# Ten of eleven FFN slabs by the seven-product scheme, with DRAM sums and four steps at other places

## The reference

```python
def reference(x, ...):
    x = first_block(x, p, norm_w, w_in, ...)
    return second_block(x, p_2, attn_norm_g_2, w_in_2, ...)

def first_block(...):                 # D_MODEL 2048, SEQ 256
    u = rmsnorm(h, norm_w[l])
    proj = jnp.einsum('bsd,dc->bsc', u, w_in[l])
    h_a = mlstm_chunkwise(q_a, k_a, v_a, i_pre, f_pre)
    y_a = jax.nn.sigmoid(ml_o) * h_a * jax.nn.silu(ml_z)
    h_b = hgrn2_chunkwise(q_b, k_b, logf_b, i_b)
    y_b = h_b * jax.nn.silu(hg_g)
    h = h + jnp.einsum('bsc,cd->bsd', y, w_out[l])
    gate = jax.nn.sigmoid(jnp.einsum('bsd,de->bse', rmsnorm(h, pe_norm_w[l]), w_pg[l]))
    h = h + gate * e
    ...
def second_block(...):                # FFN_HIDDEN 5632
    proj = h @ w_in[i]
    y_a = chunked_spatial_gating(u, v_sgu, w_s[i], b_s[i])
    y_b = stick_breaking_attention(q, k, v_att)
    merged = jax.nn.sigmoid(g_a) * (y_a @ w_up_a[i]) + jax.nn.sigmoid(g_b) * (y_b @ w_up_b[i])
    x = x + merged @ w_o[i]
    hid = rmsnorm_2(x, ffn_norm_g[i]) @ w_ffn_in[i]
    gate, up = hid[..., :FFN_HIDDEN], hid[..., FFN_HIDDEN:]
    x = x + (jax.nn.silu(gate) * up) @ w_ffn_out[i]
    ple = p[i] @ w_ple[i]
    x = x + jax.nn.sigmoid(rmsnorm_2(x, ple_norm_g[i]) @ w_ple_gate[i]) * ple
```

## Time and profile before

| what | value |
|---|---|
| median of three runs (lowest, highest) | 1894.37 us (1893.72, 1894.42) |
| the profiled execution | 1893.05 us |
| its span, first to last instruction | 1891.3 us |
| mean granted clock | 0.999 |
| busy: PE, DVE, ACT, POOL | 1877.2, 1471.8, 1140.8, 130.4 us |
| DMA, mean | 283 GB/s moved |

### The profile page before, as it was taken

How to read it: one execution, slowest core, us unless ns; L and a number is a source line. 1 busy time by engine, 2 the same in 40 slices (tenths; PEclk the granted TensorE clock), 3 DMA queues, 4 the chain that set the end, 5 groups by cost and what they waited for, 6 DMA issues and landing times.

```text
span 1891.3 us, 23371 instructions
## 1 busy us (share of the span) xinstructions
PE 1877.2 (99%) x9018; PEld 1641.9 (87%) x9018; DVE 1471.8 (78%) x1591; ACT 1140.8 (60%) x1417; POOL 130.4 (7%) x156
## 2 busy tenths in 40 slices
PE   9999999999999999999999999999999999999998
PEld 8888888888888888888888888888888888888887
DVE  6889776655666677778888657988998999898865
ACT  7556445555566556566766455666766676666553
POOL 4000011000001100000000000000000000000000
PEclk9999999999999999999999999999999999999999
DMA  9799898999989879998797886788878887987653
GB/s 392 267 284 310 274 309 272 330 347 327 309 290 312 271 269 299 321 315 278 295 313 247 330 256 239 254 311 284 276 254 320 280 271 257 327 260 249 219 188 130
DMA packets 86815, 535.95 MB, mean 283 GB/s; under 512 B 10416, under 2 KB 11184, under 8 KB 40752
## 3 DMA queue, kind: packets, MB, share of 16 engines
q1 hardware_dynamic: 72736, 458.69, 63.3%
q0 software_dynamic: 13824, 75.50, 20.6%
q10 hardware_dynamic: 144, 0.26, 0.0%
HBM read 529.69 MB, written 105.38 MB: 336 GB/s over the span
## 4 chain that ended last, share of the span: by engine, by line
PE 90%; DVE 5%; DMA 3%; issue 1%; ACT 1%; POOL 0%; SPq 0%; ACTq 0%; DVEq 0%; POOLq 0%
PE acc L1359 44%; PE acc L1364 22%; PE aux L1724 12%; PE aux L1728 6%; DVE wlo L2556 2%; PE aux L1338 2%; DMA ple<-in_w_ffn_in 1%; DVE wlo L1876 1%; PE aux L1431 1%; DVE ple L2551 1%; DMA ple<-in_w_in 1%; DMA raw<-summed 1%; PE aux L1805 0%; ACT whi L928 0%; ACT whi L1177 0%
## 5 line engine op out<-in xcount | busy, mean ns | idle before, releaser
L1876 DVE TENSOR_TENSOR wlo<-raw,whi 128x1024 fp32r<-128x1024 f32 x512 | 623.8, 1226 | 296.4 <-ACT whi L928 288.4
L928 ACT ACTIVATE whi<-raw 128x1024 fp32r<-128x1024 f32 x511 | 534.0, 1054 | 449.8 <-PE acc L1364 414.1
L1359 PE MATMUL acc<-whi,actA_hi 128*128 128x512 f32 x892 | 344.0, 386 | 0.7 <-ACT whi L928 0.7
L1359 PE MATMUL acc<-whi,actA_lo 128*128 128x512 f32 x892 | 339.1, 380 | 0.0
L1359 PE MATMUL acc<-whi,actB_hi 128*128 128x512 f32 x796 | 304.5, 383 | 0.2 <-DVE actB_lo L2673 0.2
L1359 PE MATMUL acc<-whi,actB_lo 128*128 128x512 f32 x796 | 301.7, 379 | 0.0
L1177 ACT ACTIVATE whi<-ple 128x1024 fp32r<-128x1024 f32 x192 | 201.0, 1055 | 139.4 <-PE acc L1364 55.6
L2556 DVE TENSOR_TENSOR wlo<-ple,whi 128x1024 fp32r<-128x1024 f32 x192 | 230.2, 1220 | 31.3 <-ACT whi L1177 28.5
L1364 PE MATMUL acc<-wlo,actA_hi 128*128 128x512 f32 x892 | 229.1, 379 | 0.0
L1364 PE MATMUL acc<-wlo,actB_hi 128*128 128x512 f32 x796 | 204.4, 379 | 0.0
L2556 DVE TENSOR_TENSOR wlo<-raw,whi 128x1024 fp32r<-128x1024 f32 x144 | 174.2, 1220 | 30.6 <-ACT whi L1177 28.9
(11 more groups left out here) (366 smaller groups left out, 2377.0 us busy)
## 6 DMA issues: line engine op xcount, KB each, us to landing
raw<-in_w_in SPq DMA_DIRECT2D x108, 1024.0 KB, 7.3
raw<-in_w_ffn_out SPq DMA_DIRECT2D x44, 1024.0 KB, 6.9
summed<-in_w_ffn_in POOLq DMA_DIRECT2D x36, 1024.0 KB, 11.6
raw<-in_w_ffn_in SPq DMA_DIRECT2D x72, 512.0 KB, 7.9
ple<-summed SPq DMA_DIRECT2D x24, 1024.0 KB, 4.9
raw<-summed SPq DMA_DIRECT2D x48, 512.0 KB, 5.4
ple<-in_w_ffn_in SPq DMA_DIRECT2D x18, 1024.0 KB, 6.9
ple<-in_w_ffn_in POOLq DMA_DIRECT2D x36, 512.0 KB, 9.9
```

Of the source, the lines that this page charges most:

```text
L928: act.activation(whi[:, g % RING], raw_piece(g), ACT.Copy).then_inc(hi_ready, 1)
L1359: pe.matmul(acc2(n)[:, t, :], act[x][:, k + c, t * P:(t + 1) * P], woven(whi, g, c), start=(p == 0 and c == 0 and x == 0), stop=False)
L1876: dve.tensor_tensor(wlo[:, g % RING], raw_piece(g), whi[:, g % RING].bitcast(F32), ALU.subtract)\
```

## The change

- **FFN.** Ten slabs (1 to 10) go by the seven-product scheme, slab 0 alone is standard. There are 13 seven-product slabs for 12 and 860 pieces for 848: 364 short ones (336) and 496 standard (512). F0 has 12 standard pieces (gate 0 and half of up 0), b3 8, b4 4, b5 to b11 8 each, and the last, b12, 12. b3 begins at g 452, b4 at 488, b5 at 520. Out pieces come as slab 0 alone ("out1"), pairs (1, 2) to (7, 8), slab 9 alone and 10 alone in the tail. `S_UPTO` sets by hand how many short pieces have been done by each standard piece in the first two blocks. Fills may stand behind a short piece.
- **DRAM sums.** 52 for 48. The four entries at g 277 to 289 are gone; those at every sixth piece from g 419 are twelve, to g 485, for four. POOL issues those from 443 on behind the power of the FFN's norm, in F0 and b3.
- **mLSTM rows.** Two of the four matmuls with `sel` come one piece later.
- **hB** is multiplied one piece later, **u_product** of uB 2 at five pieces after its slab for three.

```diff
@@ -91,24 +91,30 @@
     (1, [("gB", 0), ("uB", 0, 0, 0, 2)]),
     (2, [("uB", 0, 0, 2, 4), ("uA", 1), ("uB", 1)]),
     (3, [("uA", 2), ("uB", 2)]),
-    (1, [("gate", 3), ("up", 3, 0, 0, 2)]),
-    (2, [("up", 3, 0, 2, 8), ("out", (0, 1), 0, 0, 4)]),
-    (4, [("out", (0, 1), 0, 4, 8), ("out", (0, 1), 2, 0, 6)]),
-    (5, [("out", (0, 1), 2, 6, 8), ("out", (3, 2), 0)]),
-    (6, [("out", (3, 2), 2), ("out", (4, 5), 0, 0, 2)]),
-    (7, [("out", (4, 5), 0, 2, 8), ("out", (4, 5), 2, 0, 4)]),
-    (8, [("out", (4, 5), 2, 4, 8), ("out", (6, 7), 0, 0, 6)]),
-    (9, [("out", (6, 7), 0, 6, 8), ("out", (6, 7), 2)]),
-    (10, [("out", (8, 9), 0), ("out", (8, 9), 2)]),
+    (1, [("up", 0, 0, 4, 8), ("out1", 0, 0), ("out1", 0, 1)]),
+    (2, [("out1", 0, 2), ("out1", 0, 3)]),
+    (3, [("out", (1, 2), 0)]),
+    (4, [("out", (1, 2), 2)]),
+    (5, [("out", (3, 4), 0)]),
+    (6, [("out", (3, 4), 2)]),
+    (7, [("out", (5, 6), 0)]),
+    (8, [("out", (5, 6), 2)]),
+    (9, [("out", (7, 8), 0)]),
+    (10, [("out", (7, 8), 2), ("out1", 9, 0), ("out1", 9, 1)]),
 ]
-FILLS = [(0, 1, 0, 0, "d"), (0, 2, 0, 1, "d"), (1, 1, 1, 0, "d"), (1, 2, 1, 1, "d"), (2, 7, 3, 0, "e"), (2, 9, 3, 1, "e"),
...
+S_UPTO = {M_GROUPS: (0, 4, 8, 18, 21, 24, 28, 28), M_GROUPS + 1: (3, 10, 18, 28)}
+FILLS = [(0, ("s", 12), 0, 0, "e"), (0, ("s", 16), 0, 1, "e"), (1, 3, 1, 0, "e"), (1, ("s", 22), 1, 1, "e"),
...
-HID_T = {0: 0, 1: 1, 2: 1, 3: 0, 4: 0, 5: 1, 6: 0, 7: 1, 8: 0, 9: 1, 10: 2}
-HID_S = [0, 1, 0, 2, 1, 0, 2, 1, 0]
+HID_T = {j: j % 2 for j in range(10)}
+HID_T[10] = 2
+HID_S = [0, 1] * 5
 OUT_LAST = 10
+LAST_OUT = [(9, 2), (9, 3)] + [(OUT_LAST, q) for q in range(4)]
 S_GROUPS = len(BLOCKS)
 S_ORDER = [(m, q) for m in ("M1", "M2", "M7", "M5") for q in range(4)] \
     + [("M6", 0), ("M6", 1), ("M3", 0), ("M6", 2), ("M3", 1), ("M6", 3), ("M3", 2), ("M3", 3)] + [("M4", q) for q in range(4)]
@@ -188,7 +196,7 @@
         self.g_ffn = self.g
         self.first["F0"] = len(self.slabs)
         self.pair = self.g // 2
-        for x in self.unit("gate", 0) + self.unit("up", 0):
+        for x in self.unit("gate", 0) + self.unit("up", 0, 0, 0, 4):
             self.add_std(x, 4)
         self.g_block = self.g_ffn + 10
         self.pair = 0
@@ -197,7 +205,7 @@
         self.plan_s_loads(range(M_GROUPS, S_GROUPS))
         self.g_tail = self.g
         self.pair = 0
-        tail = [("ple", 0, q, 0) for q in range(4)] + [("out1", OUT_LAST, q, p) for q in range(4) for p in range(2)]
+        tail = [("ple", 0, q, 0) for q in range(4)] + [x for j, q in LAST_OUT for x in self.unit("out1", j, q)]
         for x in tail:
             self.add_std(x, 4)
         self.after.update({(S_GROUPS, t): self.g_tail + t for t in range(len(tail))})
@@ -215,7 +223,7 @@
         for t, x in enumerate(std):
             self.after[c, t] = self.g
             self.add_std(x, 2)
-            upto = max(0, min(28, t * 28 // (len(std) - (1 if c == M_GROUPS - 1 else 3))))
+            upto = S_UPTO[c][t] if c in S_UPTO else min(28, t * 28 // (len(std) - (1 if c == M_GROUPS - 1 else 3)))
             while done < upto:
                 self.add_s(c, done)
                 done += 1
@@ -464,7 +472,6 @@
         summed = nc.dram_tensor("summed", (4 * S_GROUPS, P, 4 * COLS), F32, kind="Internal").ap()
         SUM_AT = [int(24 + SUM_STEP * i) for i in range(int(116 // SUM_STEP) + 1)] + [144 + 8 * i for i in range(7)]
         SUM_AT += [199 + int(5.4 * i) for i in (0, 1, 2, 3, 8, 9, 10, 11, 12, 13)]
-        SUM_AT += [PLAN.g_plan + 1 + 4 * i for i in range(4)]
         SUM_AT += [PLAN.g_out + 11 + 6 * i for i in range(4 * S_GROUPS - len(SUM_AT))]
 
         acc = ctx.enter_context(nc.psum_tensor("acc", [P, 4, COLS], F32))
@@ -897,7 +904,7 @@
                                 pool.wait_ge(lo_ready, S_AT[c, before, q] + 1)
                                 pool.dma_start(r1[:, q], s_weights(c, what, q), accum_op=ALU.add).then_inc(sem(f"r1_added{q}"), 16)
                 if name == "ffn":
-                    add_in_dram(len(SUM_AT))
+                    add_in_dram(len([g for g in SUM_AT if g < PLAN.g_ffn]))
                 pool.wait_ge(pow_in, i + 1)
                 pool.tensor_tensor(rstd[:, i, 0:n], var[:, i, 0:n], minus_half[:, 0:n], ALU.pow).then_inc(pow_out, 1)
@@ -1490,12 +1497,13 @@
                         ins = pe.transpose(bank(u)[:, x * 8 + t * 4:x * 8 + t * 4 + 4], hrow[:, row, t * P:(t + 1) * P],
                                            ident[0:4, 0:4])
                 ins.then_inc(aux_full, 1)
-                for i in range(2):
-                    u = AUX[("bc", i)]
-                    free(u)
-                    for h in range(2):
-                        ins = pe.matmul(bank(u)[:, h * S:(h + 1) * S], sel[:, 2 * i + h, :], hrow[:, 3, :], start=True, stop=True)
-                    ins.then_inc(aux_full, 1)
+
+            def ml_rows_spread(i):
+                u = AUX[("bc", i)]
+                free(u)
+                for h in range(2):
+                    ins = pe.matmul(bank(u)[:, h * S:(h + 1) * S], sel[:, 2 * i + h, :], hrow[:, 3, :], start=True, stop=True)
+                ins.then_inc(aux_full, 1)
 
             def ml_scores():
                 pe.wait_ge(sem("ml_qk"), 2)
@@ -1550,6 +1558,9 @@
                         ml_gates_tr()
                     if (s, p) == (10, 7):
                         ml_cols()
+                        ml_rows_spread(0)
+                    if (s, p) == (11, 0):
+                        ml_rows_spread(1)
                     if (s, p) == (11, 4):
                         ml_scores()
                     for h in range(4):
@@ -2245,7 +2256,7 @@
                         if w == L0 + 27:
                             dve.wait_ge(sem("ss_hB"), half + 1)
                             variance(f"hB{half}", HG_E)
-                        if w == L0 + 30:
+                        if w == L0 + 31:
                             powered(dve, f"hB{half}")
                             x = ob[:, :, half * 512:(half + 1) * 512].rearrange("p t (h c) -> p t h c", h=4)
                             link(dve.tensor_tensor(x, x, per_head(f"hB{half}").unsqueeze(3).to_broadcast([P, T, 4, P]), ALU.mult))
@@ -2628,7 +2639,8 @@
                         gate_taken(PLAN.ffn_slab[role, j, 0])
                 for j in range(4):
                     for role in ("uA", "uB"):
-                        if g == slab_end(role, j) + (2 if slab_end(role, j) in PLAN.block_end else 3):
+                        last = slab_end(role, j)
+                        if g == last + (2 if last in PLAN.block_end else 5 if (role, j) == ("uB", 2) else 3):
                             u_product(role, j)
                 for c in range(M_GROUPS):
                     if g == S_AT[c, "M2", 3] + 3:
```

10 lines of the change are left out of this document (6 added, 4 removed), and 8 rows, old and new, of the table FILLS.

## The result

The changed kernel takes 1963.83 us (median of five, 1956.09 to 1970.65) for 1893.72 us, a ratio of 1.0372 (95% interval 1.0352 to 1.0391). It is 70 us slower; the forecast was 27 us slower, and the range ended at 1950. The profiled execution is the fastest of the five: 1956.09 us with a span of 1954.2, 62.9 more than before.

What follows compares the result with a forecast made beforehand. PE was taken as the bound (1877.2 of 1891.3 us busy), DMA close by. 1893.05 - 9.8 (small gains) + 28 (late sums) + 8.4 (M4 additions) = 1919.7, plus 1.3 for the median: 1921 us; range 1902 to 1950.

Steps and rivals of the forecast that it cites:

- the two mechanisms: DMA work of the late sums holding up F0 to b4, and M4 additions landing late in b5 to b11.
- the small terms: Five gains: fewer matmuls 5.2, clock 1.8, hB 0.9, u_product 0.9, early sums 1.0; together -9.8 us.
- the M4 additions: b5 to b11: 1.3 us less cover for the last addition, about 1.2 us new stall a block, +8.4 us (2 to 14).
- Fewer matmuls: Whole kernel: 8136 matmuls for 8160, 24 x 0.216 us less on PE, -5.2 us in full.
- Clock, hB, u_product: Half clock at 276.4 to 279.8 us gone, -1.8; PE waits near 161 and 1028 us gone, -0.9 each.
- Early sums gone: First merge block: 32.6 us of DMA work leaves, the 0.66 us stall and half the other waits go, -1.0 us.
- The late sums: F0 to b4's end: eight sums make DMA's work 164.8 us against PE's 136.6, +28 us (20 to 38).
- DVE's form_lo against M1 in b3: Short pieces M1 meet form_lo at b3's beginning: up to 2.9 us, counted as zero because DMA holds it up there anyway.
- The rivals: Queues not full, 1895 us (0.07); neither term holds, 1887 (0.10); queues block each other, 1946 (0.09); clock still falls, +1.8.
- (3): SP stands at copies waiting for sums, loads behind them blocked, DMA share 0.92: +53 for +28, 1946 us, chance 0.09.
- the forecast of +16: F0 to b4 at the skill's 358 GB/s: 54.5 MB take 152 us, late sums' term +16, time 1909 us.

Runs made afterwards that it cites:

- three_orders: The kernel before with only the spread mLSTM rows, hB one piece later and u_product of uB 2 two pieces later: 1892.04 us, ratio 0.9987.
- before_late: The kernel before with only the sums moved: the four at g 277 to 289 gone, eight at 419 to 461; 1898.71 us, ratio 1.0027.
- no_add: The changed kernel without its last eight DRAM sums and without the M4 additions in the FFN blocks: 1900.11 us, ratio 1.0035.
- after_m4: The changed kernel, all sums in place, with b5 to b11's standard pieces moved, two between the last M4 addition's issue and use: 1935.42 us, ratio 1.0210.

## Why the prediction was right or wrong

**Slower, and where:** right. b3 to b4 and the seven blocks behind are the places that it named, and it named the two mechanisms. It was wrong in size, 27 us for 70. By the profiled executions 36.3 us are missing: b5 to b11 lost 27.2 more than before where the forecast had 8.4, b3 and b4 43.2 where it had 28, and the small terms came to 2.3 less than their 9.8. The other 6.4 us are the median, which stands 7.7 above this execution and not 1.3. So two terms were too small, the M4 additions by most.

**Fewer matmuls, -5.2:** right; the stages without stalls (b12, J) are at their matmuls' time.

**Clock, hB, u_product, -3.6:** the stalls and the half clock are gone, but the whole was -2.0 (three_orders). **Early sums gone, -1.0:** too small; the first merge block won 2.4 us in the changed kernel and 2.7 in before_late. Of the smaller stalls behind the one shown, which the term took at half, one of 0.2 us is left.

**The late sums, +28:** right in size: 25.8 us by profiles, 31.3 by medians, of which the copies alone are 0.6. That the size came out is in part luck. I set the work against PE's time up to b4's end. In fact DMA is full (1.01) through F0, b3 and the first stall of b4, and then partly idle, so that b4 has a share of 0.83 as a whole: what waits are b4's first loads, not its last, and what DMA has free behind them gives nothing back. A sum to b3's end, with 130.8 us of DMA work (20 MiB of loads, four additions, eight sums) to 89 of PE, would have shown the wait where it came, though at 42 us it is too large for it: 19.5 us were lost to b3's end. The clock's falls, 1.9 us in b3 and 3.1 in b4, weren't in the sum. The share of 0.80 that it gives for b3 before is that of 1163 to 1240 us, a quarter of it F0; b3 itself was at 0.85.

**The M4 additions, +8.4:** the term that failed. b5 to b11 lose 27.7 us, for 0.5 before. Without the late sums they lose 32.6, of which 25.1 go with the additions (no_add), and b4, which I had left out, has 7.2. The last addition of b7 in the timeline of the changed kernel, POOL, PE, ACT and PE:

```profile
1487.43 0.86 POOL L905 DMA_DIRECT2D ple<-in_w_ffn_in  x1 [2.62 <-DVE wlo L2567]
...
1496.44 0.59 PE L1739 MATMUL aux<-wlo,actA_hi 128*128 128x512 f32 x2
...
1498.94 1.06 ACT L1184 ACTIVATE whi<-ple 128x1024 fp32r<-128x1024 f32 x1 [3.98 <-DMA ple<-in_w_ffn_in]
...
1500.05 0.48 PE L1735 MATMUL aux<-whi,actA_hi 128*128 128x512 f32 x1 [3.02 <-ACT whi L1184]
```

The last two matmuls ahead, 0.216 us each, end at 1496.87, which is 9.4 us behind the issue. In the earlier trace rows (it is the last of b3's four additions that they show, not the first, as their heading says) the same distance was 11.75 us, since PE's last two matmuls ahead were these, ending at 1237.72, and M4's first came at 1237.87:

```profile
1237.29 0.59 PE L1728 MATMUL aux<-wlo,actA_hi 128*128 128x512 f32 x2
```

So the cover shrank by 2.3 us, where pieces counted gave 1.3: the issue comes 1.0 us later against PE as well. DVE releases the addition, and does a second operation for each M6 piece; that it falls back because fewer standard pieces give it time fits the order of its queue, but was not tested by itself. The landing took 11.5 us for 10.8. Together that is 3.0 us more, and the stall is 3.2 us for 0.15. b7's is one of the two longest; over the seven blocks these waits are 1.7 to 3.1 us, 15.5 in all. The clock fell behind two of the seven, and the slower clock cost 4.3 us there. Moving the same eight pieces (after_m4) takes most of this away.

**What was not in the sum:** some 11 us in b3 and b4 that stay without sums and additions (5.4 and 5.5 by no_add): DVE's form_lo against M1 in b3, which I had put at "up to 2.9 us" and then at zero, since the DMA wait would hide it, two waits for wlo of 1.1 and 1.3 us later in b3, and waits for `summed` and wlo in b4, where 28 short pieces have only four standard ones. In the trace those at M1 come ahead of the DMA wait, and are not hidden.

**The rivals.** None came. (3), at 1946, was nearest in size, but its mechanism, SP standing at copies and a share of only 0.92, isn't what is seen: SP stood at one for 1.8 us in all, and the share is 1.01 in b3. The 358 GB/s of the Trainium skill (DMA: Bandwidth & Descriptors, Where 436 GB/s comes from) were too good for this mixture: at a full share F0 and b3 moved 337 and 323 GB/s, though 5 us in them read 385 and 429; and the forecast of +16 from it would have been further off than the one from rows. The same page's rule of turns between queues (Queues, rings and completion order) is tested by no run here.

## What to carry to other kernels

Set the DMA work of a stretch against the time to the first load that needs it, not to the stretch's end, and look at where in the order a deferred transfer stands; a mean share of 0.84 doesn't mean that a transfer fits in. Here a transfer of 8.15 us cost 6.3 us even at one to a block, half of it as waiting and much of the rest by the clock that fell behind the waits. When a DMA's issue waits for an engine that is nearly full, moving filler pieces changes its issue and its use: work out the distance on both engines. Where a tuned order has a latency just covered, making each block shorter by a few standard pieces takes it from the cover first, and the place of those left matters more (27 us here) than the matmuls saved (5 us).

## What the runs showed of the hardware

Over the traces of all kernels PE waited 27 times for 3.0 us or more, and 25 of these waits had a stretch with a granted clock of 0.50 at or right behind their end, with matmuls 0.43 us apart, which costs up to 1.7 us each (two waits, of 3.02 and 3.06 us, had none). Some shorter waits had one too, such as one of 2.2 us at 1743.8 us in the changed kernel. The kernel with one sum a block had a mean granted clock of 0.985 and the kernel before 0.999.

Eight copies of a MiB between other loads cost 0.6 us over two blocks, and accumulations of the same size, to the same places, the rest of 25.8 us. Beside them loads that the page has at a median of 4.8 to 8.2 us took 17 to 23 us to land. An accumulating DMA of 512 KB onto `ple` took 6.3 to 11.6 us from issue to landing in the changed kernel.

The changed kernel's five runs spread over 14.6 us, the kernel before's over 1.7 in five and over 6.2 in sixteen. The kernel with one sum a block, which waits most, spread over 4.0 in four, so the spread doesn't simply follow the waiting.
